# Reordering the query, compression and adaptive-sum work at the head of a sparse-attention layer

## The reference, cut to what matters

```python
k_cmp = silu(blocks(kv[:, :, 0] + pe_k) @ w1_k) @ w2_k      # compress(), and the same for v_cmp
q     = (h @ w_qg)[..., :1024] * 64 ** -0.5                 # four column steps of 256
gates = sigmoid((h @ w_qg)[..., 1024:])                     # 48 columns
o = gates0 * softmax(q k_cmp) v_cmp + gates1 * softmax(q k_slc) v_slc + gates2 * softmax(q k_win) v_win
h = h + o @ w_o
```

## Time and profile before

| | us |
|---|---|
| median of three runs | 961.37 |
| lowest and highest run | 959.64, 964.77 |
| profiled execution, its own time | 963.65 |
| span of that execution, first to last instruction | 961.8 |
| PE busy in the span | 945.5 (98%) |
| DVE busy | 711.6 (74%) |
| ACT busy | 490.2 (51%) |

### The profile page before, as it was taken

The page is one execution under the profiler, slowest core; times in us unless marked ns, Lnnn a source line. Parts: engine busy times, 40 slices in busy tenths (PEclk is TensorE's granted clock), DMA queues, the critical chain, the costliest instruction groups (busy, mean ns, idle before and its releaser), DMA issues.

```text
span 961.8 us, 19359 instructions
## 1 busy us (share of the span) xinstructions
PE 945.5 (98%) x7852; PEld 911.6 (95%) x7852; DVE 711.6 (74%) x1135; ACT 490.2 (51%) x717; POOL 87.0 (9%) x132
## 2 busy tenths in 40 slices
PE   8999999999999999899999999999999999999998
PEld 8999999999999887599999999999998999999998
DVE  5896877777769878968777777698876767556554
ACT  6344644443347557846444443548667655433441
POOL 7000000000000042420000000020000000000000
PEclk9999999999999999999999999999999999999999
DMA  9746758686845662047586868436345347654611
GB/s 283 257 175 228 255 203 294 231 299 208 288 140 176 227 219 89 1 136 258 198 290 228 293 224 291 138 117 190 123 141 175 126 153 249 204 190 145 235 57 44
DMA packets 129835, 186.97 MB, mean 194 GB/s; under 512 B 6384, under 2 KB 100976, under 8 KB 129776
## 3 DMA queue, kind: packets, MB, share of 16 engines
q1 hardware_dynamic: 122000, 159.69, 50.1%
q0 software_dynamic: 6912, 25.17, 7.5%
q10 hardware_dynamic: 864, 1.29, 0.4%
HBM read 185.09 MB, written 1.05 MB: 194 GB/s over the span
## 4 chain that ended last, share of the span: by engine, by line
PE 89%; DVE 4%; ACT 3%; DMA 2%; issue 1%; SPq 1%; DVEq 0%; ACTq 0%
PE ps L1915 45%; PE ps L1993 19%; PE ps L1911 13%; PE ps L1913 4%; DMA g_raw<-in_a_w_in 2%; ACT g_hi L685 1%; PE ps L2123 1%; PE ps L2070 1%; PE ps L2188 1%; PE ps L2203 1%; SPq L528 0%; DVE g_lo L1192 0%; ACT opb_hi L703 0%; ACT e_odd L899 0%; PE ps L2315 0%
## 5 line engine op out<-in xcount | busy, mean ns | idle before, releaser
L1915 PE MATMUL ps<-opa_hi,g_hi 128*128 128x256 f32 x864 | 225.1, 283 | 2.0 <-ACT g_hi L685 1.2
L1915 PE MATMUL ps<-opa_lo,g_hi 128*128 128x256 f32 x864 | 216.5, 279 | 0.0
L1915 PE MATMUL ps<-opa_hi,g_lo 128*128 128x256 f32 x864 | 178.9, 280 | 0.0
L1310 DVE TENSOR_TENSOR g_lo<-g_raw,g_hi 128x2048 fp32r<-128x2048 f32 x54 | 123.8, 2292 | 69.3 <-ACT g_hi L759 69.3
L1915 PEld LDWEIGHTS ps<-opa_hi,g_hi 128*128 128x128 f32 x864 | 162.5, 188 | 5.6 <-issue 3.0
L1915 PEld LDWEIGHTS ps<-opa_lo,g_hi 128*128 128x128 f32 x864 | 159.2, 188 | 0.1
L1993 PE MATMUL ps<-hid_hi,d_hi 128*128 128x256 f32 x528 | 148.6, 281 | 0.0
L1993 PE MATMUL ps<-hid_lo,d_hi 128*128 128x256 f32 x528 | 148.4, 281 | 0.0
L1993 PE MATMUL ps<-hid_hi,d_lo 128*128 128x256 f32 x528 | 148.4, 281 | 0.0
L1192 DVE TENSOR_TENSOR g_lo<-g_raw,g_hi 128x2048 fp32r<-128x2048 f32 x54 | 123.5, 2289 | 29.6 <-ACT g_hi L685 26.9
L1915 PEld LDWEIGHTS ps<-opa_hi,g_lo 128*128 128x128 f32 x864 | 135.6, 188 | 0.0
(11 more groups left out here) (339 smaller groups left out, 1807.8 us busy)
## 6 DMA issues: line engine op xcount, KB each, us to landing
g_raw<-in_f_w_gu SPq DMA_DIRECT2D x44, 1024.0 KB, 8.9
ada_raw<-in_w_ada POOLq DMA_DIRECT2D x48, 512.0 KB, 6.4
d_raw<-in_f_w_down SPq DMA_DIRECT2D x22, 1024.0 KB, 5.1
g_raw<-in_w_in SPq DMA_DIRECT2D x14, 1024.0 KB, 8.4
g_raw<-in_w_gate SPq DMA_DIRECT2D x11, 1024.0 KB, 7.3
g_raw<-in_w_up SPq DMA_DIRECT2D x11, 1024.0 KB, 9.7
d_raw<-in_w_down SPq DMA_DIRECT2D x11, 1024.0 KB, 5.2
g_raw<-in_a_w_in SPq DMA_DIRECT2D x8, 1024.0 KB, 7.5
```

Source lines behind the costliest of these rows:

```text
L1310: dve.tensor_tensor(part_view(g_lo, g0 + r, True), raw_cols(c % 2, r % 2, True), part_view(g_hi, g0 + r, True).bitcast(F32), ALU.subtract) ...
L1915: mm = pe.matmul(pair(b)[:, a, :], wt[:, a * P:(a + 1) * P], xt, **st)
```

## The change

- The chunk order becomes KV, QG and QG+1, compression of keys, compression of values, QG+2 and QG+3: the first query weights come before the compression's.
- Both compressions use bank 7 (`CMP_BANK`). `cmp_hidden(0)` moves from behind KV+4 to behind the gate columns, and it first waits until KV+5 has been emptied out of bank 7. `cmp_hidden(1)` moves from ahead of the first scores into QG+1, behind its second of eight units, and waits until the keys' result has been read. The second layer of both (`compressed_heads`) comes behind QG+1.
- `scores(0)` comes right behind QG, the keys' turn and the gates' turn; it no longer waits for the adaptive sums. `ada_rows(0)` moves behind the units of WO+1, ahead of WO+2, and `make_mod(0)` into `add_product(WO, ...)` on DVE, behind the second `ada_pair` and ahead of the addition of WO+3.
- On DVE, `split_g(QG)` and `split_g(QG+1)` come ahead of the gate product; `cmp_blocks(1)` comes behind the first compression; heads 0 to 3 are shifted, and 0 and 1 normalized, ahead of `split_g(QG+2)`, `evac_q(1)` and the compressed keys' copies.
- On ACT, `split_g(QG)` and `split_g(QG+1)` move forward; the exponentials of heads 0 and 1 come ahead of the values' compression; one small activation asks for the exponential ahead of them.
- `bias_h` gets a place of its own over a mask that is made later; POOL no longer waits for the compression before the first biases.

```diff
@@ plan_chunks
     steps(KV, 6, False)
+    steps(QG, 2, False)
     chunks.append(("cmp", 0))
-    steps(QG, 2, False)
     chunks.append(("cmp", 1))
@@ gpsimd
-            pool.wait_ge(cmp_hid_done, 2)
             for h in range(NH):
@@ scalar
             split_g(KV + 5)
             key_copies(2)
+            split_g(QG)
             key_copies(4)
+            split_g(QG + 1)
-            tokens_copy(0)
-            split_g(QG)
...
-            split_g(QG + 1)
             act.wait_ge(gate_scaled, 1)
             act.activation(gate_row, gate_row, ACT.Exp, scale=-1.0).then_inc(gate_exp, 1)
...
+            act.activation(small[:, 12:14], eps[:, 0:2], ACT.Exp)
             exps(0, 0)
             exps(0, 1)
+            tokens_copy(1)
+            split_g(QG + 2)
+            act.wait_ge(cmp_turned, 2)
...
@@ vector, add_product
                     ada_pair(0 if first == AO else 1, 0, s - 1)
+                if s == 2 and first == WO:
+                    make_mod(0)
@@ vector, key and value steps
-                if s == 4:
-                    dve.wait_ge(cmp_hid_done, 1)
-                    cmp_blocks(1)
+                if s >= 4:
+                    split_g(QG + s - 4)
                 if s == 5:
...
                 if s >= 4:
-                    split_g(QG + s - 4)
                     ada_pair(0, 5, s - 2)
...
+            dve.wait_ge(cmp_hid_done, 1)
+            cmp_blocks(1)
             evac_q(0)
-            make_mod(0)
+            shift(0)
+            shift(1)
...
+            normalize(0)
+            normalize(1)
+            shift(2)
+            shift(3)
+            split_g(QG + 2)
+            evac_q(1)
             dve.wait_ge(kc_done, 1)
...
-            shift(0)
-            shift(1)
-            split_g(QG + 2)
-            normalize(0)
-            shift(2)
-            shift(3)
-            evac_q(1)
-            normalize(1)
             compressed_shift(0)
             split_g(QG + 3)
@@ tensor
             def cmp_hidden(w):
...
+                if w == 0:
+                    pe.wait_ge(g_evac, evacs(KV + 5))
+                else:
+                    pe.wait_ge(cmp_hid_silu, 1)
...
-                if s == 4:
-                    cmp_hidden(0)
-            cmp_turn(0)
...
             mm.then_inc(gate_done, 1)
+            cmp_hidden(0)
             g_step(QG, opb_hi, opb_lo, no_wait)
-            cmp_hidden(1)
-            ada_rows(0)
-            cmp_turn(1)
+            cmp_turn(0)
...
             pe.wait_ge(g_evac, evacs(QG))
-            pe.wait_ge(ada_turned, 1)
             scores(0)
-            g_step(QG + 1, opb_hi, opb_lo, no_wait, ks=range(5))
+            g_step(QG + 1, opb_hi, opb_lo, no_wait, ks=range(2))
+            cmp_hidden(1)
+            g_step(QG + 1, opb_hi, opb_lo, no_wait, ks=range(2, 5))
             scores(1)
+            cmp_turn(1)
             g_step(QG + 1, opb_hi, opb_lo, no_wait, ks=range(5, KT))
+            compressed_heads()
             query_units(0, 3)
...
             out_units(1, 2, 6)
+            pe.wait_ge(shifted, NH)
+            ada_rows(0)
             for s in (2, 3):
```

More of the change, by code:

```diff
@@ L169, in layer_kernel @@
     any_vis = sb("any_vis", [P, TT])
+    over_d = ExitStack()
+    bias_h = sb("bias_h", [P, 2, 384], on=over_d)
+    over_d.close()
     dil_count = sb("dil_count", [P, 384])
@@ L229, in layer_kernel @@
     over_x.close()
-    bias_h = sb("bias_h", [P, 2, 384], on=over_b)
-    sb("pad_h", [P, 1024 - 768], on=over_b)
+    sb("pad_h", [P, 1024], on=over_b)
     vc_blk = sb("vc_blk", [P, NH, HD], on=over_b)
@@ L367, in layer_kernel @@
     vrep = gu[:, 1, :, :]
-    mod_rows = (e_odd[:, 1, :], gu[:, :, :, :].rearrange("p a b t -> p (a b t)")[:, 0:768])
+    mod_rows = gu[:, :, :, :].rearrange("p a b t -> p (a b t)")[:, 0:768]
+    CMP_BANK = 7
     fold = pt_buf[:, 0:64]
@@ L660, in _ @@
             load_ada(26, 48)
+            pool.wait_ge(shifted, NH)
             const(pool.memset(dil_mask[:, :], 1.0))
@@ L870, in _ @@
             key_copies(2)
+            split_g(QG)
             key_copies(4)
+            split_g(QG + 1)
             def tokens_copy(w):
                 act.wait_ge(cmp_hid_done, w + 1)
-                act.activation(hid_tok(w), ps[:, w, 0:256], ACT.Copy).then_inc(cmp_tok_copied, 1)
-            tokens_copy(0)
-            split_g(QG)
-            act.wait_ge(cmp_turned, 1)
-            act.activation(hid_cmp[:, 0, :, :, :].rearrange("p a g n -> p (a g n)"), ps[:, 0, 256:384],
-                           ACT.Silu).then_inc(cmp_hid_silu, 1)
-            split_g(QG + 1)
+                act.activation(hid_tok(w), ps[:, CMP_BANK, 0:256], ACT.Copy).then_inc(cmp_tok_copied, 1)
             act.wait_ge(gate_scaled, 1)
             act.activation(gate_row, gate_row, ACT.Exp, scale=-1.0).then_inc(gate_exp, 1)
[L885 to L890, removed]
-            split_g(QG + 2)
+            tokens_copy(0)
+            act.wait_ge(cmp_turned, 1)
+            act.activation(hid_cmp[:, 0, :, :, :].rearrange("p a g n -> p (a g n)"), ps[:, CMP_BANK, 256:384],
+                           ACT.Silu).then_inc(cmp_hid_silu, 1)
+            act.activation(small[:, 12:14], eps[:, 0:2], ACT.Exp)
             def exps(j, e):
@@ L904, in _ @@
             exps(0, 1)
+            tokens_copy(1)
+            split_g(QG + 2)
+            act.wait_ge(cmp_turned, 2)
+            for a in range(2):
+                src = ps[:, CMP_BANK, 256 + a * 64:256 + (a + 1) * 64].rearrange("p (g n) -> p g n", g=NG)
+                act.activation(vrep[:, a, :].rearrange("p (g h n) -> p g h n", g=NG, h=4),
+                               src.unsqueeze(2).to_broadcast([P, NG, 4, 16]), ACT.Silu).then_inc(cmp_hid_silu, 1)
             exps(1, 0)
@@ L1274, in make_mod @@
         def make_mod(half):
-            n, rows32 = 24 * half, mod_rows[half]
+            n, rows32 = 24 * half, mod_rows
             dve.wait_ge(ada_summed, half + 1)
@@ L1518, in evac_q @@
                                               in1=r_both, op0=ALU.mult, op1=ALU.mult), g)
-            evac_q(0)
-            make_mod(0)
[L1522 to L1536, removed]
             def normalize(h):
@@ L1584, in compressed_factors @@
                 dve.tensor_tensor(c4(x), c4(x), f.unsqueeze(2).to_broadcast([P, 16, 16]), ALU.mult).then_inc(cs_made, 1)
+            dve.wait_ge(cmp_hid_done, 1)
+            cmp_blocks(1)
+            evac_q(0)
             shift(0)
             shift(1)
-            split_g(QG + 2)
+            dve.wait_ge(gate_turned, 1)
+            dve.tensor_copy(gates[:, :, :], ps[:, 6, 256:352].rearrange("p (a n) -> p a n", a=TT)).then_inc(gates_copied, 1)
+            dve.wait_ge(gates_copied, 1)
+            own(dve.tensor_scalar(gates[:, :, :], gates[:, :, :], 1.0, None, ALU.add))
+            own(dve.reciprocal(gates[:, :, :], gates[:, :, :]))
             normalize(0)
+            normalize(1)
             shift(2)
             shift(3)
+            split_g(QG + 2)
             evac_q(1)
-            normalize(1)
+            dve.wait_ge(kc_done, 1)
+            dve.wait_ge(consts, c_block1)
+            dve.wait_ge(kc_zeroed, 1)
+            for b in range(2):
+                dve.tensor_copy(kc_blk[HD * b:HD * b + HD, :, b, :],
+                                ps[HD * b:HD * b + HD, 7, 0:64].rearrange("p (g n) -> p g n", g=NG)).then_inc(kc_made, 1)
+            for half in range(2):
+                v = ps[:, 7, HD * (1 + half):HD * (2 + half)].unsqueeze(1).to_broadcast([P, 8, HD])
+                dve.tensor_tensor(vc_blk[:, 8 * half:8 * half + 8, :], v, blk16.unsqueeze(2).to_broadcast([P, 8, HD]),
+                                  ALU.mult).then_inc(kc_made, 1)
             compressed_shift(0)
@@ L1985, in ffn @@
                 sum_squares(norm)
+            if f == 1:
+                pe.wait_ge(ada_turned, 1)
             def d_step(i, r, s):
@@ L2069, in cmp_hidden @@
                     q = 64 * (l % 2)
-                    mm = pe.matmul(ps[q:q + 64, w, 0:256], b_cmp[:, l, :, :].rearrange("p g n -> p (g n)"),
+                    mm = pe.matmul(ps[q:q + 64, CMP_BANK, 0:256], b_cmp[:, l, :, :].rearrange("p g n -> p (g n)"),
                                    w1_view(c % 2)[:, l, :], start=(l < 2), stop=(l >= 14), skip_group_check=True)
@@ L2078, in cmp_turn @@
                 for a in range(2):
-                    mm = pe.matmul(ps[:, w, 256 + 64 * a:320 + 64 * a], hid_tok(w)[:, a * P:(a + 1) * P], fold,
+                    mm = pe.matmul(ps[:, CMP_BANK, 256 + 64 * a:320 + 64 * a], hid_tok(w)[:, a * P:(a + 1) * P], fold,
                                    start=True, stop=True, skip_group_check=True)
@@ L2144, in _, with compressed_heads @@
             mm.then_inc(gate_turned, 1)
[L2145 to L2152, removed]
-                for a in range(2):
-                    mm = pe.matmul(ps[:, 7, HD * (1 + half):HD * (2 + half)], vrep[:, a, half * P:(half + 1) * P],
-                                   w2_v[:, a, :], start=(a == 0), stop=(a == 1))
```

(12 more changed lines are left out.)

## The result

After the change the median is 965.86 us (963.31 to 966.94, 17 runs), against 961.39 (959.64 to 964.77, 17 runs) before. The ratio is 1.0043, with an interval of 1.0034 to 1.0051: 3.3 to 4.9 us more, 4.1 in the middle. In the middle that is less than the 0.5% (4.8 us) which the prediction set as the bound of no change, on its slower side; the upper end of the interval just reaches it. The forecast was +2.65 us. The profiled execution of the changed kernel took 966.17 us, with a span of 964.4 and a mean clock of 1.000; that of before had 961.8 and 0.998.

The account below looks back on a forecast made before the run. PE was taken to bound the program, so only its waits and slow stretches count. QG's end +0.8, to the first turn +0.45, attention 0, `make_mod` +1.39: +2.65 us, 964.0 on the median; 8 in 10 range 958.5 to 967.5.

Parts of the forecast that it names:

- the two large waits: PE waits of 2.6 us ahead of `cmp_hidden(0)` and about 1.6 us for operand tile 6 in F1.
- The wait for the bank: Ahead of `cmp_hidden(0)`, PE waits 2.6 us until DVE empties KV+5 from bank 7, replacing the old 1.83 us wait.
- query weights first: At QG: its weights go out at 306.83 instead of 320.06, so PE's 1.83 us wait for them goes.
- The values' weights: Rival, chance 0.06: the values' compression weights land late, near 344; three microseconds later costs +3 us, perhaps the clock: 967 to 969.
- Small waits to the first turn: Between QG's end and `turn(0, 0)`: 0.1 us after `scores(0)`'s evacuation and 0.35 behind DVE's chain after `scores(1)`, +0.45 together.
- The attention: From 380 to 410: earlier scores gain 0, PE keeps its 3.9 us idle; bounds 0 and 3.9.
- a lead that survives: Rival, chance 0.12: DVE or ACT stays ahead into attention, closing PE's 3.9 us of idling: -1.25 us, 960.1.
- The sums: Ahead of WO+2: `ada_rows(0)` moves its 1.43 us at no gain; `make_mod(0)`, no longer hidden, costs +1.39 in F1.
- The clock: Around QG: 1.79 us lost at half clock behind PE's wait, priced the same before and after; bounds 0 and 1.79.
- clock lost in both: At QG's end: the 1.79 us clock loss counted in the old and new kernel alike, leaving +0.8 there.
- The rivals on the clock: No loss behind the 2.6 us gap, chance 0.20: +0.9, 962.2; loss also at F1's wait, 0.14: +4.4, 965.8.

Follow-up runs that it names:

- KV+5 first: Changed kernel with DVE emptying KV+5 ahead of the split of QG and the adaptive pair: 965.32 us, ratio 1.0036 to the kernel before.
- QG first: Changed kernel with QG ahead of `cmp_hidden(0)` and the keys' turn behind `scores(0)`: 963.91 us, ratio 1.0021 to the kernel before.
- the slot freed early: Kernel of "all together", with DVE splitting QG and QG+1 ahead of emptying KV+5 and ACT's QG+2 split behind the values' Silu: 963.57 us, ratio 1.0014.
- all together: Changed kernel with QG ahead of `cmp_hidden(0)`, `make_mod(0)` behind WO+3's addition, QG+2's split ahead of two shifts, QG+3's ahead of head 2's exponentials: 961.89 us, ratio 1.0003.
- the sums late alone: Kernel before with only `ada_rows(0)` and `make_mod(0)` moved to their new places: 965.97 us, ratio 1.0046.
- `make_mod` behind: Kernel before with `ada_rows(0)` moved late and `make_mod(0)` behind the addition of WO+3: 963.54 us, ratio 1.0018.

## Why the prediction came out as it did

The direction, the places of the two large waits and the range were right; the size was 1.5 us too small.

**The wait for the bank** was forecast at 2.6 us and is 2.47, ended by the instruction that was named. What stood behind it was not seen. I took 6.9 us as the landing of the keys' weights, by which they were covered at 327; but that figure is the median of two transfers. The rows had a better one: the chunk that went out at the same moment before, QG's at 320.06, held ACT until 329.27, 9.2 us. By it the keys' weights come 1.5 us behind the gates' end. In the runs they come only 0.5 us before the bank (KV+5 first: a wait of 1.96 in place of 2.47), so the cure of the wait that I blamed gives no time that can be told from none. The wait belongs to the order of the transfers as much as to that of DVE. Three edits, KV+5 first, QG first and the slot freed early, each moved it to the next chunk: keys' weights, values' weights, QG+2. This is where the gain of "query weights first" went. There are two slots, each chunk must wait until the one two places before it has been read out, and in each of these three orders, and in the one of before, PE has a wait of 1.6 to 2.0 us for one of the chunks. The values' weights, a rival of its own in the prediction, were in time in the changed kernel: its list has no wait for them.

The Trainium skill, in "Trainium Kernel Development and Optimization", Key Constraints, says that transfers issued from SP, ACT and POOL run on the same DMA engines and interleave. The 9.9 us, beside a load of `w_ada`, agree with it.

**Small waits to the first turn** were 0.45 in the sum. This term was mis-sized, and its step misplaced: the compressed copies that I saw last in DVE's chain came in time, and it is the split ahead of them, behind `shift(2)` and `shift(3)`, that held PE by 0.77 us. With the split put ahead of the shifts that wait is gone ("all together"). Two more small waits were not in the sum: 0.2 us ahead of the gates, and 0.15 more than before in F1+1.

**The attention** was given 0, and is 63.64 us against 63.66. The chance of a lead that survives falls: scores that start 8.3 us sooner do not matter, as the prediction argued from what DVE and ACT have done by the first turn; the equal length is shown, the reason is not tested by itself. The windows from 380 to 410 (the columns of the earlier trace rows),

```profile
380.00:390.00 10.00, 9.35 (x76) 6.61 (x74) 9.68 (x36) 9.19 (x27) 2.50 (x3) 1.00 0.00 0
390.00:400.00 10.00, 8.21 (x70) 5.21 (x68) 9.75 (x48) 8.38 (x34) 3.75 (x3) 1.00 0.01 2
400.00:410.00 10.00, 8.56 (x68) 5.63 (x66) 9.06 (x43) 9.10 (x34) 7.87 (x11) 1.00 0.00 1
```

leave PE 3.88 us idle, 3.9 before.

**The sums.** `ada_rows` costs the same 1.43 us. `make_mod` was forecast to lengthen F1's wait from 0.19 to 1.6 us; it is 1.65, and goes back to 0.3 when `make_mod` stands one place later. What I costed at nothing, the old place of `ada_rows`, was not empty: alone, the move uncovers 1.0 us of ACT's work. In the whole change this is hidden again, since each turn has units of QG+1 or scores ahead of it: no such wait is in its list.

**The clock** was the step that failed in its reasoning, though it added nothing to the sum: I counted 1.79 us of loss in every run of both kernels. It comes in some runs only. Over 69 runs of the kernel before, 30 have a mean clock below 0.999, with a mean span of 960.8 us against 959.4 of the others: 1.4 us. Of 22 runs of the changed kernel, 17 are below it, with 964.0 against 962.9. So "clock lost in both" was wrong in each direction: the loss is not certain, and it was more frequent, 77% of the runs against 43%, which is 0.34 times 1.4, about 0.5 us. (Of those 22 runs 17 were timed in other rounds than the 69; in the rounds that have both it is 4 of 5 against 8 of 23, which is little to go by.) That the term stood on both sides and dropped out of the sum is luck. The rivals on the clock were both put as all or nothing, and neither is what happens; behind the 1.65 us in F1 neither trace has a slow stretch. The profiled execution of before had a loss and the one of after had none, so that their spans do not differ by the 3.22 us of the waits: 3.22 - 1.79 + 1.0 of the last store is 2.4, of 2.6.

A second estimate weighs the clock in every run: its span times what its mean clock lacks of 1, which is the time lost if PE bounds the slow stretch. That is 1.2 us in the mean of the 69 runs before and 1.8 in the 22 after, 0.6 us more. Against the kernel before in the same rounds it is 2.1 us more with the sums late alone, 1.3 with `make_mod` behind, 2.0 with the slot freed early, and 0.3 less with QG first. So half of the first one's rise, nearly all of the second's, and more than all of the third's is clock: by the estimate that order would beat the kernel before by 0.7 us at an equal clock, which no run shows directly.

Where the new waits are 3.22 us and the clock 0.5, the sum is 3.7. The mean spans of those 22 and 69 runs are 963.7 and 960.0, 3.7 us apart as well, and the measured 3.3 to 4.9 holds it. On the prediction's own sum that is: bank +0.64 (forecast +0.8), small waits +0.8 to the first turn (+0.45), 0.2 at the gates and 0.15 in F1+1 (0), F1 +1.46 (+1.39), clock +0.5 (0).

What stays open is what decides in a run whether the clock falls. It is not the length of one wait alone: 2.47 us passed without a loss in one trace and not in the other. Nor is it that wait alone: filled with matmuls, the changed kernel still has 5 of 8 runs below 0.999, the kernel before 5 of 12, and with QG first it is 2 of 11. The Trainium skill, in "TensorE: Matmul & The Clock Gate", HAM oscillation, would let a gap of this size pass; the second trace does not agree. Three experiments had a slow stretch from 384 to 392 in the attention, at waits that the other kernels have there too. The Trainium skill, in the section "A second HAM failure mode" of the same page, tells of another kernel in which frequent short idle moments between groups of matmuls brought it about. No run here shows that they were the cause.

## What to carry to other kernels

Where weights go through a ring of two slots, the order of the chunks decides only which of them is late; look for the chunk that takes the place of the one that was moved forward, and for how long its slot is held, before counting the old wait as won. Before a step is moved away, ask what ran behind it: the 1.43 us of column sums covered a copy and a Silu on ACT that no list of waits showed. And a short instruction put into a chain that has no slack, as `make_mod` ahead of the last addition, cost its whole length here, and one place later nearly nothing.

## What the runs showed of the hardware

Unexpected was that the granted clock differs from run to run of one unaltered program: 30 of 69 runs have a mean clock below 0.999 and are 1.4 us longer in the mean than the others, and of two traces of one kernel one has a slow stretch behind a wait of 2.5 us (clock 0.79 and 0.78 in two windows of 4 us) and the other has none (1.00). A single trace can therefore show a slow stretch that other runs do not have, and a price read from it is to be weighed by how often it occurs. The same holds for the last store: 3.7 us to land in one trace of the changed kernel, 2.7 in the other.
